# Three unrounded half chunks, ten products of zeros and a later low-rank gate at the start of a two-block kernel

## The reference, cut

```
def gla_mixer(x, w_in, w_gate_up, b_gate, norm_g, w_out):
    proj = x @ w_in
    q, k, v, r, g_lr = jnp.split(
        proj, [GLA_DK, 2 * GLA_DK, 2 * GLA_DK + GLA_DV, 2 * GLA_DK + 2 * GLA_DV], axis=-1)
    log_a = jax.nn.log_sigmoid((g_lr @ w_gate_up + b_gate).astype(jnp.float32)) / GLA_TEMP
...
    bcum = jnp.cumsum(to_chunks(log_a, H), axis=3)
    q_e = q * jnp.exp(bcum)
    scores = jnp.einsum('bhnik,bhnjk->bhnij', q_e, k * jnp.exp(-bcum))
    scores = jnp.where(causal_mask(), scores, 0.0)
    o_intra = jnp.einsum('bhnij,bhnjv->bhniv', scores, v)
...
    o = head_norm(o, norm_g, H) * jax.nn.silu(r.astype(jnp.float32))
    return o @ w_out
```

## Time and profile before

| | |
|---|---|
| median of 3 runs | 1576.06 us (1575.84 to 1578.87) |
| the profiled execution | 1574.67 us, span from first to last instruction 1572.8 us |
| busy share of the span | PE 96%, PEld 71%, DVE 59%, ACT 41%, POOL 2% |
| mean granted TensorE clock | 0.972 |
| HBM | 418.26 MB read, 267 GB/s over the span |

### The profile page before, as it was taken

How to read it: one execution, slowest core, us unless ns; L and a number is a source line. 1 busy time by engine, 2 the same in 40 slices (tenths; PEclk the granted TensorE clock), 3 DMA queues, 4 the chain that set the end, 5 groups by cost and what they waited for, 6 DMA issues and landing times.

```text
span 1572.8 us, 20875 instructions
## 1 busy us (share of the span) xinstructions
PE 1504.9 (96%) x8534; PEld 1111.9 (71%) x8534; DVE 922.9 (59%) x1583; ACT 639.6 (41%) x1046; POOL 39.2 (2%) x39
## 2 busy tenths in 40 slices
PE   7999999998999999997798999999999999999998
PEld 6876343336988534432688878889887877889897
DVE  4985111118896411113998768987868856765554
ACT  6443121114334312212555645444455556454443
POOL 0000000000000000000300000000001000000000
PEclk9999999999999999999899999999999999999999
DMA  9877999995564999999556334998935522435540
GB/s 359 314 309 317 422 422 421 422 421 199 214 268 177 421 421 421 422 421 390 214 186 216 132 137 172 340 353 322 339 136 182 186 86 83 159 136 186 188 161 27
DMA packets 58776, 420.75 MB, mean 268 GB/s; under 512 B 6625, under 2 KB 6689, under 8 KB 8370
## 3 DMA queue, kind: packets, MB, share of 16 engines
q1 hardware_dynamic: 58034, 417.19, 67.7%
q0 software_dynamic: 640, 2.14, 0.4%
HBM read 418.26 MB, written 1.05 MB: 267 GB/s over the span
## 4 chain that ended last, share of the span: by engine, by line
PE 81%; DVE 11%; ACT 6%; issue 1%; DMA 0%; SPq 0%; DVEq 0%; ACTq 0%
PE ps L784 79%; ACT AR L1817 3%; DVE lo L1914 2%; DVE AR L1907 2%; ACT hi L1476 1%; PE ps L870 1%; DVE ACC L1907 1%; PE ps L1362 1%; DVE AR L1904 1%; PE ps L1099 1%; PE ps L1336 1%; ACT AR L1829 0%; DVE TINY L1904 0%; DVE AR L2541 0%; ACT AR L1725 0%
## 5 line engine op out<-in xcount | busy, mean ns | idle before, releaser
L1914 DVE TENSOR_TENSOR lo<-raw,hi 128x1024 fp32r<-128x1024 f32 x300 | 365.7, 1240 | 110.5 <-ACT hi L1476 109.4
L1476 ACT ACTIVATE hi<-raw 128x1024 fp32r<-128x1024 f32 x300 | 310.2, 1056 | 197.1 <-PE ps L784 191.1
L784 PE MATMUL ps<-T,hi 128*128 128x256 f32 x1792 | 332.2, 287 | 10.6 <-DVE lo L1914 8.4
L784 PEld LDWEIGHTS ps<-T,hi 128*128 128x128 f32 x1792 | 283.4, 193 | 22.1 <-DVE lo L1914 9.5
L784 PE MATMUL ps<-hi,T 128*128 128x512 f32 x896 | 288.6, 398 | 3.9 <-DVE T L1907 3.0
L784 PE MATMUL ps<-T,lo 128*128 128x256 f32 x896 | 254.7, 284 | 0.0
L784 PEld LDWEIGHTS ps<-hi,T 128*128 128x128 f32 x896 | 170.4, 190 | 41.0 <-issue 5.3
L784 PE MATMUL ps<-lo,T 128*128 128x512 f32 x448 | 176.2, 393 | 0.0
L784 PEld LDWEIGHTS ps<-T,lo 128*128 128x128 f32 x896 | 173.0, 193 | 0.0
L784 PE MATMUL ps<-hi,AF 128*128 128x512 f32 x512 | 166.1, 396 | 0.5 <-DVE AF L2662 0.5
L1907 DVE SCALAR_TENSOR_TENSOR AR<-AR,ps 128x512 f32<-128x512 f32 x52 | 35.5, 685 | 175.6 <-ACT AR L1647 108.1
(11 more groups left out here) (240 smaller groups left out, 1844.6 us busy)
## 6 DMA issues: line engine op xcount, KB each, us to landing
raw<-in_moe SPq DMA_DIRECT2D x76, 1024.0 KB, 14.8
raw<-in_b_ff SPq DMA_DIRECT2D x64, 1024.0 KB, 5.0
AR<-in_moe SPq DMA_DIRECT2D x60, 1024.0 KB, 13.4
raw<-in_ada SPq DMA_DIRECT2D x48, 1024.0 KB, 5.5
ring<-in_moe SPq DMA_DIRECT2D x44, 1024.0 KB, 13.9
raw<-in_b_in SPq DMA_DIRECT2D x24, 1024.0 KB, 6.8
raw<-in_b_gate SPq DMA_DIRECT2D x16, 1024.0 KB, 4.8
ACC<-in_moe SPq DMA_DIRECT2D x12, 1024.0 KB, 16.3
```

Source lines behind the costliest of these rows:

```text
L784: return e.matmul(o, l, r, start=a, stop=z, skip_group_check=True)
L1476: e.activation(hi[n % NC][:, :], raw[place[c]][:, 1024 * half:1024 * half + 1024], ACT.Copy).then_inc(*to("hi", "hi", n))
L1914: tt(lo[n % NC][:, :], r, hi[n % NC][:, :], SUB).then_inc(*to("lo", "lo", n))
```

## The change

The first chunk's two halves and the first half of the second chunk are no longer rounded: `whole` gives 3, 1, 0, 0 for the four chunks of q and k, and `block_a` gets `F` and waits for the tokens' landing for such units. SP issues chunk 1 ahead of `vec`, and chunk 2 and `wgu` ahead of `cst`. GpSimd fills a place of 384 columns (`BLANK`, where the r gate is written later) with zeros before its other fills; PE begins with ten fp32 products of it, into a bank that nobody reads. `prepare` gets two empty steps in front.

```
     def prepare():
+        yield []
+        yield []
         yield [("glr",), ("constants",)]
...
-            VV, SR = ar(7168, 2, 1024), ar(9216, 2, 1024)
+            VV, SR, BLANK = ar(7168, 2, 1024), ar(9216, 2, 1024), ar(9216, 384)
...
-            def block_a(name, job, kt, xs, th, tl, freed_by, x=None):
+            def block_a(name, job, kt, xs, th, tl, freed_by, x=None, whole_xs=None):
...
                     if k % 2 == 0:
-                        w.wait_ge(*after(*xs[k // 2]))
+                        w.wait_ge(*after(*(whole_xs if whole_xs and l is None else xs)[k // 2]))
...
+                w.wait_ge(*after("blank"))
+                p = take("warm")
+                for _ in range(10):
+                    mm(p[:, 0:256], m.BLANK[:, 0:128], m.BLANK[:, 128:384], True, True)
+                free.append(bank["warm",])
                 for what, *a in walk_gla(feed):
                     if what == "qk":
-                        block_a("qk", a, 8, xs, TH, TL, ("qk_out", a[0]))
+                        block_a("qk", a, 8, xs, TH, TL, ("qk_out", a[0]), F, [("x_t", g // 2) for g in range(4)])
...
             def gla():
                 m = gla_mem
+                e.memset(m.BLANK, 0.0).then_inc(*to("gla_fill", "blank"))
                 e.memset(m.KM[:, :, 0, 64:128], 0.0).then_inc(*to("gla_fill"))
...
             load(0, 1024)
+            load(1)
             e.dma_start(vec[:, :], D["vec"]).then_inc(*landed("vec"))
-            load(1)
-            e.dma_start(cst[:, :], D["cst"]).then_inc(*landed("cst"))
             load(2)
             e.dma_start(gla_mem.WG, D["wgu"]).then_inc(*landed("wgu"))
+            e.dma_start(cst[:, :], D["cst"]).then_inc(*landed("cst"))
...
     if name == "ml_qk":
         return 2
+    if name == "gla_qk":
+        return (3, 1, 0, 0)[c]
     return 3 if name.startswith("moe") else 0
```

## The result

Five executions of the changed kernel took 1584.03 to 1588.40 us, median 1585.76; five of the kernel before, beside them, had a median of 1577.83. The ratio is **1.0063, interval 1.0047 to 1.0080**: slower by 10 us by this ratio, by 7.9 between the two medians. The forecast was slower by 4.5 us, 1580.6, with a range to 1584.0: the direction held, the size did not. The profiled execution (1588.40, span 1586.2) is the slowest of the five; what is read from it here is read at single places.

A forecast was written before the change was run, and what follows sets the result against it. PE was taken to bound the kernel until 96 us, at 81% of the last-ending chain. Start -1.9, mask wait +4.7 and clock +1.7 sum to +4.5 us on a median of 1576.06: 1580.6 us, range 1576.0 to 1584.0.

The forecast's parts named there:

- start: PE's work up to the gate's second product ends at 26.5 instead of 28.46: gain 1.9 us, from 1.2 to 2.6.
- wait for the last mask: Before the first product with values, PE waits for DVE to mask the fourth head's scores: 4.7 us, range 3.0 to 5.2.
- clock right behind: After PE's wait for the mask the clock falls to 0.50, losing 1.7 us, ends 0 and 3.4.
- behind the second stop: After PE's stop for the second transposes (98.56 before), nothing takes the delay back and the rest stays as before: 0.
- My 4.7 is nearer to 3.47, so I take 1.7: Clock loss after the mask wait, sized by the 3.47 us wait at 912.00, not the harmless 1.50 at 98.56: 1.7 us.
- a few tenths: Allowance for the spread of the runs, added to the ends +0.4 and +7.4, giving 1576.0 to 1584.0 us.
- the lag ahead of the first mask could shrink: DVE's 2.64 us lag before the first mask could fall by up to 1.1, cutting PE's wait from 5.2 to 4.1.
- rival 3: At the start, products of zeros do not raise the clock: +8.8, 1584.9 us; chance 0.08.
- DVE does not catch up: Opposite of a rival: DVE catches up by the third mask, wait 3.0, sum +0.4, 1576.5 us; chance 0.13.
- swallows the delay: Rival: expert-layer loads that don't wait for PE absorb the delay: +0, 1576.1 us; chance 0.05.

The follow-up runs named there:

- values_later: The changed kernel with three empty steps ahead of the values, so two units stand between last scores and first values; 0.9995 of the kernel before.
- gate_only: The kernel before with only the two empty steps in front of the low-rank gate added; 1.0043 of the kernel before.
- after_again: The changed kernel itself, measured once more with nothing altered; 1.0065 of the kernel before, median 1584.94 us beside 1575.47.
- no_zeros: The changed kernel with three empty steps ahead of the values, without the zero fill and its ten products; 0.9996 of the kernel before.
- one_step: The changed kernel with one empty step instead of two in front of the low-rank gate; 1.0023 of the kernel before.
- start_only: The changed kernel without the two empty steps; zeros, unrounded units and new load order stay; 0.9997 of the kernel before.

## Why the prediction was wrong

| term of the sum | forecast | profiled execution | the runs |
|---|---|---|---|
| start | -1.9 | -1.0 | -1.5 at the stop of values_later, its time (0.9995) not clear of noise |
| wait for the last mask | +4.7 | +5.41 | 5.40 to 5.42 in three runs |
| clock right behind | +1.7 | +2.8 | 2.75 (with and without zeros in the wait); 1.9 in gate_only, 2.6 in after_again |
| behind the second stop | 0 | +5.9 | 2 to 3 us by the medians, cause open |

The place, the engine, the cause of the wait and the fall of the clock came as forecast. **The step that failed is the size of the clock term**: "My 4.7 is nearer to 3.47, so I take 1.7". What a fall costs is half of the PE work that meets the low stretch. At 912 that work took 3.4 us; here PE came back 5.7 us before the stretch ended, and 2.75 us went, as the run with zeros in the wait shows. One row could not give the size: where the stretch begins within the wait differs from execution to execution (gate_only lost 1.9, after_again 2.6, in the same wait). The forecast counted the two ends, 0 and 3.4, into its range.

The other terms erred to the same side: the wait by 0.7, the start by 0.4 to 0.9. At the second stop this makes 7.5 us where 4.5 were forecast. For what lies behind it, "the rest as before", there was no term; there the runs leave 2 to 3 us open. And the sum was put on a median of 1576.06, while the five executions of before beside the change had 1577.83: 1.8 of the 5.2 us between 1580.6 and 1585.76 are that. The forecast's range gave "a few tenths" to a scatter that 30 executions of the kernel before show to be 1570.8 to 1581.1.

*The wait.* Its working gave 5.2, the runs 5.4. I took 4.7 because the lag ahead of the first mask could shrink. It grew: the first mask began 2.98 us after its scores had given way (58.56 to 61.54), 2.64 before; 2.98 + 14.23 - 12.34 + 0.55 is the wait, 5.4 (12.34 is PE's way from the first scores to the last, 57.23 to 69.57). DVE has no gap in this stretch at all.

*The start.* The zeros ended at 7.15 to 8.49 in the seven runs that have ten of them, 7.9 in the mean, which is what I took; the profiled execution had the latest end. The rest was dearer by 0.4: units, low-rank product, rounded unit and gate product took 18.98 instead of 18.6. That zeros bring the rise of the clock forward is shown: a trace's own list of clock changes begins at the rise, at 4.3 to 7.1 us with ten zeros, 5.1 to 7.2 with five, 9.7 in no_zeros, 11.9 in gate_only and 14.4 in the kernel before. It holds nothing ahead of that, so the 1.00 that the earlier trace rows show there is no reading, and does not speak against the pace. That the earlier rise makes the kernel faster is not shown by any time here.

*The rivals.* Zeros do raise the clock (rival 3 is wrong; its time, 1584.9, came out near by other terms). DVE does not catch up. Nothing in the expert layer swallows the delay. The Trainium skill (TensorE: Matmul & The Clock Gate, "HAM oscillation — how this bites in real kernels") had the rule that decided the sign of the third term: a kernel whose PE waits between bursts pays for warming each time. This case agrees, with 2.75 us at one wait, and the runs show a way out beside shorter waits: 0.9988 without fills in eight later waits of 1.6 to 3.5 us, 0.9930 with them.

## What to carry to other kernels

Before a chain is moved by a few units, look at what its last step then stands next to on the slowest engine in order: here one unit later was free of that wait, two cost 5.4 us, and moving the consumer along made it free again. Warming products ahead of the first real ones moved the rise of the clock, but ten, five or none of them made no difference that the times can tell. Where PE must wait and its next bank is already free, unread products in that wait kept its clock and did not delay what came behind them (the first values start at 76.37 with the zeros in the wait, at 76.42 without); where the bank was not free, they came late, and two batches cost some 6 us each.

## What was not expected of the hardware

The rise of the clock is no fixed time after PE's first product: ten zeros from 1.20 on ended anywhere from 7.15 to 8.49 us, and with the same start the level rose at 14.4 us in the kernel before and at 11.9 in gate_only. The clock can fall with PE hardly stopped: at 24.8 in one_step behind products that use 16 columns or 17 rows of the array and one wait of 0.23 us (start_only has the same products, with a wait of 2.26 us ahead of them, and no fall there), and near 130 in every kernel among 1-column products. And products of zeros held the clock as real ones do: 1.00 through a wait of 5.3 us that otherwise took it to 0.50.
